# Two edits in a layer's first mixer: the mLSTM normaliser becomes the 129th column of the matrix memory, and the softmax division of the windowed attention moves from VectorE to GpSimd

## The reference

```python
p = softmax(concat([s_loc, s_ctx, s_sink]))
out = p[..., :w3] @ v_window + p[..., w3:w3 + nctx] @ v_context
```

```python
num = s @ v + a[..., None] * (cm @ q)
den = sum(s, axis=-1) + a * (nv @ q)
h = num / maximum(abs(den), exp(-m_row))[..., None]
c_new = decay * cm + einsum('bhl,bhlv,bhlk->bhvk', wt, v, k)
n_new = decay * nv + einsum('bhl,bhlk->bhk', wt, k)
```

## Time and profile before

| what | us |
|---|---|
| three runs | 4887.66, 4886.40, 4867.94 |
| median | 4886.4 |
| the profiled execution | 4881.98 |
| its span | 4880.3 |
| TensorE busy | 4299.8 (88%) |
| VectorE busy | 1847.9 (38%) |
| ScalarE busy | 992.6 (20%) |
| GpSimd busy | 230.5 (5%) |

### The profile page before, as it was taken

One profiled execution on the slowest core, in us unless ns is written; L12 is line 12 of the kernel. 1 busy time (PEld: TensorE's weight loads), 2 busy tenths in 40 slices (PEclk: granted clock), 3 DMA queues, 4 the chain that ended last, 5 costly groups with the idle time before them and its releaser, 6 DMA issues. The chain is left out here.

```text
span 4880.3 us, 37835 instructions
## 1 busy us (share of the span) xinstructions
PE 4299.8 (88%) x13778; PEld 2229.9 (46%) x13778; DVE 1847.9 (38%) x3380; ACT 992.6 (20%) x1918; POOL 230.5 (5%) x273
## 2 busy tenths in 40 slices
PE   8999998497889699888685999997989995999996
PEld 4444444493444354447542444443444442444443
DVE  3556551544758323463463111103634246101111
ACT  3434441154010311261210000003110002000001
POOL 0011010200000000000000000000000000000000
PEclk9999999698999799896797999998999997999998
DMA  4121213546545112004327999972011113999995
GB/s 108 54 69 61 86 63 109 139 122 224 155 126 176 57 56 80 5 1 135 102 66 270 319 318 318 324 262 79 30 41 40 36 44 110 360 318 315 313 318 203
DMA packets 529503, 733.47 MB, mean 150 GB/s; under 512 B 127846, under 2 KB 242374, under 8 KB 529352
## 3 DMA queue, kind: packets, MB, share of 16 engines
q1 hardware_dynamic: 517608, 688.50, 42.1%
q0 software_dynamic: 11744, 43.00, 3.2%
HBM read 655.40 MB, written 76.01 MB: 150 GB/s over the span
## 5 line engine op out<-in xcount | busy, mean ns | idle before, releaser
L2545 PE MATMUL ps<-ffn_w,moe_xT 128*128 128x512 f32 x2048 | 888.8, 595 | 3.3 <-DVE moe_xT L2606 3.3
L504 PE MATMUL ps<-hT,pr_w 128*128 128x512 f32 x1536 | 671.3, 595 | 4.9 <-issue 3.5
L2545 PEld LDWEIGHTS ps<-ffn_w,moe_xT 128*128 128x128 f32 x2048 | 390.7, 191 | 495.6 <-issue 491.6
L504 PEld LDWEIGHTS ps<-hT,pr_w 128*128 128x128 f32 x1536 | 290.6, 191 | 364.4 <-issue 361.7
L2561 PE MATMUL ps<-moe_w,moe_hT 128*128 128x512 f32 x1024 | 444.9, 592 | 0.1
L2619 DVE TENSOR_TENSOR moe_sg<-moe_sg,ps 128x512 f32<-128x512 f32 x64 | 44.0, 688 | 837.8 <-PE ps L2545 837.8
L2561 PEld LDWEIGHTS ps<-moe_w,moe_hT 128*128 128x128 f32 x1024 | 192.1, 190 | 230.1 <-issue 230.1
L3077 PE MATMUL ps<-hA,abp_w 128*128 128x512 f32 (+1 forms) x624 | 252.3, 565 | 0.6 <-DVE bv L3190 0.6
L2586 ACT ACTIVATE moe_sg<-ps 128x512 f32<-128x512 f32 x64 | 38.2, 597 | 1008.2 <-PE ps L2545 1008.2
L2884 PE MATMUL ps<-hG,gmu_w 128*128 128x512 f32 x512 | 226.2, 600 | 5.1 <-DMA gmu_w<-in_gm_w_in 5.1
L2631 DVE SCALAR_TENSOR_TENSOR moe_ye<-ps,moe_gc,moe_gt 128x512 f32<-128x512 f32 x64 | 48.0, 751 | 388.4 <-PE ps L2561 388.4
(11 more groups left out here) (648 smaller groups left out, 5752.9 us busy)
## 6 DMA issues: line engine op xcount, KB each, us to landing
ffn_w<-in_moe_w_gate SPq DMA_DIRECT2D x64, 2048.0 KB, 10.3
ffn_w<-in_moe_w_up SPq DMA_DIRECT2D x64, 2048.0 KB, 9.1
moe_w<-in_moe_w_down SPq DMA_DIRECT2D x64, 2048.0 KB, 10.6
pr_w<-in_w_in SPq DMA_DIRECT2D x24, 1024.0 KB, 5.6
wout_modw<-in_w_mod SPq DMA_DIRECT2D x48, 512.0 KB, 3.9
ple_modw<-in_w_mod SPq DMA_DIRECT2D x48, 512.0 KB, 4.8
X<-scratch_grow SPq DMA_DIRECT2D x48, 256.0 KB, 5.0
X<-scratch_k SPq DMA_DIRECT2D x32, 256.0 KB, 3.4
```

The costliest lines, as they stand in the source:

```text
L504: ins = eng.matmul(C.ps[r % NRING][:, :], w[:, (n // 2) % NW, k, (n % 2) * P:(n % 2 + 1) * P], HT[:, k, half * BANK:(half + 1) * BANK], st ...
L2545: ins = eng.matmul(C.ps[2 + b][:, :], xT[:, k, :], wb[b][:, k, :], start=(k == 0), stop=(k == KD - 1))
```

## The change

In `stage_mlstm` the value tiles `vs` and the state `Cst` get 129 columns for each head. The last column of the value tiles is set to 1.0 once, by four small memsets on GpSimd ahead of its loop, and TensorE waits for them (`s_one`) before its first instruction. The normaliser is the last column of `Cst`; `Nst`, the matmuls L3407, L3408 and L3414 and the instructions L3478, L3480 and L3440 go. Since 4 x 129 columns don't fit a PSUM bank of 512, the numerator lies in two banks (a for heads 0 and 1, the next one for heads 2 and 3), and the update in banks b and c. So L3463, L3465 and L3470 each become two instructions, one for each bank. The value loads write rows of 128 into rows of 129.

In `stage_attn` VectorE keeps only the sum and the reciprocal (`sums`, now for block n-1 at the end of its block n); GpSimd does the eight divisions of a block and raises `s_p`.

```diff
@@ -3301,7 +3301,7 @@
 
-def stage_mlstm(nc, C, S, name, steps, fwd_at, bwd_at, Cst, Nst, HX, first):
+def stage_mlstm(nc, C, S, name, steps, fwd_at, bwd_at, Cst, HX, first):
 
@@ -3323,14 +3323,20 @@
 
-        ks, qs, vs = ([two(f"{x}{par}", [P, GH, P]) for par in g2] for x in ("k", "q", "v"))
+        ks, qs = ([two(f"{x}{par}", [P, GH, P]) for par in g2] for x in ("k", "q"))
+        vs = [two(f"v{par}", [P, GH, P + 1]) for par in g2]
         bcs = [two(f"bc{par}", [P, 2, GH, P]) for par in g2]
         s_ld = [sems(f"load{par}") for par in g2]
-        s_kT, s_qk, s_kw, s_df, s_DT, s_sd0, s_SD, s_qa, s_nm, s_up, s_h, s_S, s_N, s_rt, s_r2 = (sems(x) for x in (
-            "kTps", "qkps", "kw", "dif", "DT", "sd0", "SD", "qa", "numps", "upps", "h", "state", "norm", "rt", "recip"))
+        s_kT, s_qk, s_kw, s_df, s_DT, s_sd0, s_SD, s_qa, s_nm, s_up, s_h, s_S, s_rt, s_r2 = (sems(x) for x in (
+            "kTps", "qkps", "kw", "dif", "DT", "sd0", "SD", "qa", "numps", "upps", "h", "state", "rt", "recip"))
         s_z = st.sem("zero")
-        a, b, c, d = ([C.ps[4 * g + i] for g in g2] for i in range(4))
+        s_one = st.sem("ones")
+        a = [(C.ps[4 * g], C.ps[4 * g + 1]) for g in g2]
+        b, c = ([C.ps[4 * g + i] for g in g2] for i in (2, 3))
+        pair = lambda bank: bank[:, 0:2 * (P + 1)].rearrange("p (h c) -> p h c", h=2)
+        numer = lambda g, h: a[g][h // 2][:, (h % 2) * (P + 1):(h % 2 + 1) * (P + 1)]
+        grown = lambda g, h: (b, c)[h // 2][g][:, (h % 2) * (P + 1):(h % 2 + 1) * (P + 1)]
         block = st.block()
@@ -3352,7 +3358,7 @@
                     eng.dma_start(k[g][:, :, :], chan(S.d["mk"])[:, :, bass.ds(t0, P)]).then_inc(s_ld[par][g], 16)
-                    eng.dma_start(v[g][:, :, :], S.d["mv"][bass.ds(t0, P), :].rearrange("t (h e) -> t h e", h=GH)).then_inc(s_ld[par][g], 16)
+                    eng.dma_start(v[g][:, :, 0:P], S.d["mv"][bass.ds(t0, P), :].rearrange("t (h e) -> t h e", h=GH)).then_inc(s_ld[par][g], 16)
                     step = n + (CTX // P if out else 0)
@@ -3373,13 +3379,17 @@
 
+            for par in g2:
+                for g in g2:
+                    eng.memset(vs[par][g][:, :, P:P + 1], 1.0).then_inc(s_one, 1)
             if out:
         def _(eng):
+            eng.wait_ge(s_one, 4)
             if first:
-                eng.wait_ge(s_z, 4)
+                eng.wait_ge(s_z, 2)
             def turn(i, par, later):
@@ -3401,17 +3411,12 @@
                         for h in range(GH):
-                            hs = slice(h * P, (h + 1) * P)
-                            eng.matmul(a[g][:, hs], SD[g][:, h, :], v[g][:, h, :], start=True, stop=False)
-                            eng.matmul(a[g][:, hs], qa[g][:, h, :], Cst[g][:, h, :], start=False, stop=True)
-                            eng.matmul(d[g][:, h:h + 1], SD[g][:, h, :], C.ones[:, 0:1], start=True, stop=False)
-                            ins = eng.matmul(d[g][:, h:h + 1], qa[g][:, h, :], Nst[g][:, h:h + 1], start=False, stop=True)
+                            eng.matmul(numer(g, h), SD[g][:, h, :], v[g][:, h, :], start=True, stop=False)
+                            ins = eng.matmul(numer(g, h), qa[g][:, h, :], Cst[g][:, h, :], start=False, stop=True)
                         ins.then_inc(s_nm[g], 1)
                     for h in range(GH):
-                        hs = slice(h * P, (h + 1) * P)
-                        eng.matmul(b[g][:, hs], kw[g][:, h, :], v[g][:, h, :], start=True, stop=True)
-                        ins = eng.matmul(c[g][:, h:h + 1], kw[g][:, h, :], C.ones[:, 0:1], start=True, stop=True)
+                        ins = eng.matmul(grown(g, h), kw[g][:, h, :], v[g][:, h, :], start=True, stop=True)
                     ins.then_inc(s_up[g], 1)
@@ -3437,8 +3442,7 @@
                     eng.memset(f(Cst[g]), 0.0).then_inc(s_z, 1)
-                    eng.memset(Nst[g][:, :], 0.0).then_inc(s_z, 1)
-                eng.wait_ge(s_z, 4)
+                eng.wait_ge(s_z, 2)
             def turn(i, par, later):
@@ -3460,24 +3464,28 @@
 
-                        eng.scalar_tensor_tensor(rt[g][:, :], d[g][:, 0:GH], -1.0, col[g][:, 2, :], ALU.mult, ALU.max).then_inc(s_rt[g], 1)
+                        den = [pair(a[g][x])[:, :, P] for x in range(2)]
+                        for x in range(2):
+                            ins = eng.scalar_tensor_tensor(rt[g][:, 2 * x:2 * x + 2], den[x], -1.0, col[g][:, 2, 2 * x:2 * x + 2], ALU.mult, ALU.max)
+                        ins.then_inc(s_rt[g], 1)
                         eng.wait_ge(s_rt[g], n * 2 + 1)
-                        eng.tensor_tensor(rt[g][:, :], rt[g][:, :], d[g][:, 0:GH], ALU.max).then_inc(s_rt[g], 1)
+                        for x in range(2):
+                            ins = eng.tensor_tensor(rt[g][:, 2 * x:2 * x + 2], rt[g][:, 2 * x:2 * x + 2], den[x], ALU.max)
+                        ins.then_inc(s_rt[g], 1)
                         eng.wait_ge(s_rt[g], n * 2 + 2)
                         dst = HX[g][:, bass.ds(at[g](n) - CTX // P, 1), :, :].rearrange("p a h c -> p (a h) c")
-                        eng.tensor_tensor(dst, a[g][:, :].rearrange("p (h t) -> p h t", h=GH),
-                                          rt[g][:, :].unsqueeze(2).to_broadcast([P, GH, P]), ALU.mult).then_inc(s_h[g], 1)
+                        for x in range(2):
+                            ins = eng.tensor_tensor(dst[:, 2 * x:2 * x + 2, :], pair(a[g][x])[:, :, 0:P],
+                                                    rt[g][:, 2 * x:2 * x + 2].unsqueeze(2).to_broadcast([P, 2, P]), ALU.mult)
+                        ins.then_inc(s_h[g], 1)
                     else:
                     for h in range(GH):
-                        hs = slice(h * P, (h + 1) * P)
-                        eng.scalar_tensor_tensor(Cst[g][:, h, :], Cst[g][:, h, :], bc[g][:, 1, h, edge:edge + 1], b[g][:, hs], ALU.mult, ALU.add)
-                    eng.tensor_tensor(Nst[g][:, :], Nst[g][:, :], bc[g][:, 1, :, edge], ALU.mult).then_inc(s_N[g], 1)
-                    eng.wait_ge(s_N[g], n + 1)
-                    eng.tensor_tensor(Nst[g][:, :], Nst[g][:, :], c[g][:, 0:GH], ALU.add).then_inc(s_S[g], 1)
+                        ins = eng.scalar_tensor_tensor(Cst[g][:, h, :], Cst[g][:, h, :], bc[g][:, 1, h, edge:edge + 1], grown(g, h), ALU.mult, ALU.add)
+                    ins.then_inc(s_S[g], 1)
 
@@ -3569,8 +3577,8 @@
         mx, nmx, ls, es, rd = ([st.sb(f"{x}{i}", [P, 2 * GH]) for i in range(NB)] for x in ("mx", "nmx", "ls", "es", "rd"))
-        s_sk, s_sc, s_el, s_ec, s_m, s_mh, s_e, s_v, s_p, s_tr, s_cp, s_pv, s_po = (
-            st.sem(x) for x in ("sink", "scores", "evloc", "evctx", "max", "headmax", "exp", "dve", "p", "turned", "copied", "pv", "out"))
+        s_sk, s_sc, s_el, s_ec, s_m, s_mh, s_rd, s_e, s_v, s_p, s_tr, s_cp, s_pv, s_po = (
+            st.sem(x) for x in ("sink", "scores", "evloc", "evctx", "max", "headmax", "recip", "exp", "dve", "p", "turned", "copied", "pv", "out"))
         block = st.block()
@@ -3671,7 +3679,7 @@
                         eng.wait_ge(s_tr, 2 * z_end[n - NB])
-                        eng.wait_ge(s_e, n - NB + 1)
+                        eng.wait_ge(s_p, n - NB + 1)
                     if at + nb < 3:
@@ -3692,28 +3700,31 @@
 
-            def shares(n, h):
-                q, lo = n % NB, blocks(n)[0][0] * P
-                if h == 0:
-                    eng.wait_ge(s_e, n + 1)
-                    step(eng.tensor_tensor(ls[q][:, :], ls[q][:, :], es[q][:, :], ALU.add))
-                    step(eng.reciprocal(rd[q][:, :], ls[q][:, :]))
-                for g in range(2):
-                    i = GH * g + h
-                    ins = eng.tensor_scalar(Sc[q][:, g, h, lo:], Sc[q][:, g, h, lo:], rd[q][:, i:i + 1], None, ALU.mult)
-                if h == GH - 1:
-                    ins.then_inc(s_p, 1)
+            def sums(n):
+                q = n % NB
+                eng.wait_ge(s_e, n + 1)
+                step(eng.tensor_tensor(ls[q][:, :], ls[q][:, :], es[q][:, :], ALU.add))
+                eng.reciprocal(rd[q][:, :], ls[q][:, :]).then_inc(s_rd, 1)
 
                         local(n, h)
-                    if n >= 2:
-                        shares(n - 2, h)
                 if n < NT:
                     maxima(n)
-            for h in range(GH):
-                shares(NT - 1, h)
+                if n:
+                    sums(n - 1)
+
+        @block.gpsimd
+        def _(eng):
+            for n in range(NT):
+                q, lo = n % NB, blocks(n)[0][0] * P
+                eng.wait_ge(s_rd, n + 1)
+                for g in range(2):
+                    for h in range(GH):
+                        i = GH * g + h
+                        ins = eng.tensor_scalar(Sc[q][:, g, h, lo:], Sc[q][:, g, h, lo:], rd[q][:, i:i + 1], None, ALU.mult)
+                ins.then_inc(s_p, 1)
 
@@ -3790,13 +3801,12 @@
         with ExitStack() as state:
```

(7 more changed lines are left out.)

## The result

Over four runs the changed kernel took a median of 4810.46 us (4809.76 to 4812.8), the kernel before on the same chip 4881.79: ratio 0.9859, 95% interval 0.9836 to 0.9882, so 71 us faster. The profiled execution took 4812.8 us with a span of 4811.1. The forecast was 4812 and "faster". That the number fits so well is partly chance: several of its terms were off, in opposite directions.

The account below looks back on a forecast made before the run. The prediction took TensorE to bound the changed stages (busy 138 of the last 147 us, 135 of attention's 171). 51 + 7 + 17 = 75 us off 4882 gave 4807, 4812 on the median's footing; 8-in-10 range 4786 to 4848.

Parts of the forecast that it names:

- One-column passes cost as much as wide ones: mLSTM on TensorE: a pass takes 0.215 us at half clock, 0.112 at full, with one column or 128.
- Warm step 10.4 us, VectorE-bound: Sequence mLSTM at full clock: TensorE needs 8.1 us, VectorE sets the pace, 10.4 us a step against 15.3.
- First step and two middle steps cold, 15.4 us each: Sequence mLSTM: these steps run at half clock, TensorE-bound; the two middle ones cost 5 us extra each.
- Gain of the steps, 51: Sequence mLSTM: steps get 51 us shorter; 61 with all middle steps warm, 27 with all cold.
- Context stage, 7: Context mLSTM: 32 removed passes and two dropped instructions gain 7 us (5 to 8).
- Attention, 17: Attention: TensorE's six waits for VectorE's divisions go, GpSimd's divisions stay hidden; gain 17 us (10 to 20).
- Value loads, memsets, contention at nothing: mLSTM value loads in 512-byte rows cost nothing, memsets hide behind first loads, no VectorE-GpSimd contention is charged.
- the half clock: Rival, 15%: the clock stays half through the mLSTM; 51 us gained in all, 4835.
- free one-column passes: Rival, 4%: the mLSTM's one-column passes were nearly free; 10 + 17 us gained, 4859.
- dear 129-column passes: Rival, 3%: mLSTM passes of 129 columns cost more; at three times, 50 us slower, 4936.
- Attention gains nothing: Rival, 14%: GpSimd's divisions exceed 2.1 us or slow VectorE through shared memory ports; 58 us gained, 4828.
- main case: Whole kernel, 62%: 4792 to 4834 us, with six to none of the middle steps warm and attention at either end.

Follow-up runs that it names:

- passes_back: The changed kernel with the one-column matmuls put back, their results unused; its sequence steps took 133.9 us.
- light_loads: The changed kernel with three of four heads of v and q set to ones once instead of loaded; 4797.06 us.
- act_out: The changed kernel with the output's scaling by the divisor moved from VectorE to ScalarE; 3.2 us gained by the medians.
- attn_only: The attention part of the change alone, the mLSTM as in the kernel before; 10.3 us gained by the medians.
- split_div: The changed kernel with the last three of a block's eight division rows given to VectorE; 4793.32 us against 4805.87 on the same chip.
- after_again: The changed kernel run once more, unchanged; 4805.87 us.

## Why the prediction was right

- **One-column passes cost as much as wide ones:** shown, by `passes_back`. The estimate by the back-to-back gap of 60 cycles (Trainium skill, "TensorE: Matmul & The Clock Gate", "Back-to-back issue gap"), 10 us for them all, is out: the mLSTM part gained 61. That section gives the figure for a matmul by itself and says that it leaves out the weight load; every pass here has one.
- **Warm step 10.4 us, VectorE-bound:** the number is right, 10.38 in `light_loads`. The bound isn't VectorE's alone: 0.6 us of it are a wait for the numerator, where the prediction had "0.5 us of semaphore lags", and `act_out` shows more waits for TensorE behind it. In the kernel after the mean was 11.36. "They just fit" was too kind to the loads, which were late in four of seven steps (2.6 us in all); the half clock cost 4.6 us in the three others.
- **First step and two middle steps cold, 15.4 us each:** mis-sized. No step was cold throughout: the first took 11.5 us, and the two middle ones in which the clock fell took 12.0, 1.6 us more than undisturbed and not 5. The steps came to 86.9 us, by the number the all-warm sum of 86, though neither all warm nor undisturbed.
- **Gain of the steps, 51:** the profiled pair gave 60. Against the four executions with 120 passes a step (146.6, 128.1, 135.7, 133.9; mean 136) the 86.9 us are 49 less. So the term is 9 too low for the pair and right for the medians, and the latter by luck: the old steps were set some 10 us too long, by a profile with three falls of the clock, and the new ones 9 us too long.
- **Context stage, 7:** with the first loads 7.3 in the pair; right. Its clock rose from 0.50 to 0.65 to 0.74, which wasn't foreseen and isn't explained; `passes_back` and `attn_only` had 0.50 again, so it goes with the passes.
- **Attention, 17:** 10.4 in the pair, 10.3 by the medians of `attn_only`. The failed step is the divisions' price: "Nearest is the one-input row; I take 0.8 to 0.9", upper bound 1.6; it was 1.89. Even the two-input row, scaled to 640 columns, lay under it. The second slip was "GpSimd has a whole block (17 us)": that holds in the middle alone; at both ends a block is 12 us. The place named as tightest, the last block, stalled for 1.7 us, but the first and the seventh for more. By the last block's maxima 16.2 us were gained; the tail lost 5.9. The Trainium skill's "1-input is roughly line-rate" ("GPSIMD Engine Reference", "Engine selection") doesn't hold for this form here: 1.89 us against VectorE's 0.55. The upper end of 20 us was too low as well: with a cheap division 23 are there.
- **Value loads, memsets, contention at nothing:** k and v now land in 4.8 and 4.6 us where it was 3.0 and 2.9, alike, so it isn't the rows of `v`; with lighter loads k was back at 3.1, so it is the fuller queue. The memsets lie behind the first loads. Contention: some 1.4 us, below.
- **Rivals:** the half clock, free one-column passes and dear 129-column passes are out. "Attention gains nothing" was half true: 1.89 us lay near its 2.1. The main case's 4792 and 4834 stand on the footing of the profiled execution; on the median's, as all other numbers, its terms give some 4 to 6 us more at either end. The result lies well inside both.
- **Signs of being wrong:** two of those it named came true. Attention's transposes waited for GpSimd, and decay tiles were lengthened by loads. Both are in the result, at 12.2 and 2.6 us.

By the medians the mLSTM part gave 61 us where 58 were forecast and attention 10 where 17 were, 71 in all for 75; and the median of before, with its fourth run, stood 4.6 us lower than the one the sum was set against (4881.8 for 4886.4). The two nearly cancel, so 4812 stood 1.5 us from the result.

## To carry to other kernels

Before a stage's gain is read from one pair of profiles, profile the old kernel again: a TensorE-bound stage at a changing clock differed by 18 us here with the same code, and the new stage, where TensorE has slack, repeated to within 2. Work moved to an idle engine hides only where its own time is shorter than the shortest interval between its jobs, first and last ones above all, and its price has to be taken from the very form of instruction. When removing passes makes another engine the bound, look at the loads and at that engine's own waits next: here both lay within 1 us a step of it. And when an experiment meets a rival's number, check that it also shows the rival's cause: `act_out` met the loads' number, and its waits were for TensorE.

## What was unexpected of the hardware

- GpSimd's multiplication by a column of scalars (`tensor_scalar`, 128x640, f32) takes 1.89 us, 3.4 times VectorE's 0.55 in `split_div`; the same product as `tensor_tensor` with a repeated second input takes 1.11.
- VectorE and GpSimd do disturb each other in some forms. In `split_div`, where both start `tensor_scalar` at the same time, VectorE's three rows take 2.02 us in place of three times 0.55, the second of them 1.09, and GpSimd's first 2.53 us; so it is in every block of 640 columns. In the kernel after, the one block whose maxima fell into GpSimd's time showed 0.69, 0.65 and 0.57 us for instructions of 0.17, and the first two did the same in `attn_only` and `after_again`. Scaling from PSUM (L3688) kept its 680 ns. Not every small instruction in GpSimd's time suffered: the second of those maxima instructions kept 0.17 us, and so did the sum of the last block (at 2170.1). That GpSimd is the cause is read from the times alone.
